# Taking the row sums of a matrix-vector product from VectorE's fused multiply-and-sum and giving the sum to ScalarE, in a float32 transformer stack on one core

## The reference, cut to what matters

```python
# first block, feed-forward: D_FF = 2816
h = rmsnorm(x, norm_ffn_g[l])
u = causal_dwconv(h @ w_up[l], ffn_conv_w[l], ffn_conv_b[l])     # 3 taps over the tokens
val, gt = jnp.split(u, 2, axis=-1)
x = x + (jax.nn.gelu(gt) * val) @ w_down[l]

# third block: 9 * 1024 = 9216 outputs from 1024 inputs
mod = (jax.nn.silu(c) @ w_ada[l] + b_ada[l]).reshape(b_, N_SUB, 3, D_MODEL)
```

## Time and profile before

| what | value |
|---|---|
| median of 3 runs | 3217.38 us (3214.98 to 3224.53) |
| the profiled execution: its time, its span | 3212.26 us, 3210.5 us |
| busy over the span: PE, DVE, ACT, POOL | 85%, 42%, 28%, 27% |
| DVE busy from 670 to 1050 us | 351.0 of 380.0 us |
| PE busy from 670 to 1050 us, granted clock | 340.2 of 380.0 us, 0.94 |
| ACT busy from 670 to 1050 us | 66.9 of 380.0 us |
| POOL busy from 670 to 1050 us | 133.3 of 380.0 us |

### The profile page before, as it was taken

The page is one execution under the profiler, slowest core; times in us unless marked ns, Lnnn a source line. Parts: engine busy times, 40 slices in busy tenths (PEclk is TensorE's granted clock), DMA queues, the critical chain, the costliest instruction groups (busy, mean ns, idle before and its releaser), DMA issues.

```text
span 3210.5 us, 30605 instructions
## 1 busy us (share of the span) xinstructions
PE 2715.9 (85%) x11642; PEld 2080.2 (65%) x11642; DVE 1344.4 (42%) x1924; ACT 910.6 (28%) x1089; POOL 882.5 (27%) x193
## 2 busy tenths in 40 slices
PE   6858588889998889998977669999978886799996
PEld 5636377677776668675754446888857543578885
DVE  3471522399999530554223442222243113323223
ACT  3322321311111333554334332212232212222211
POOL 2202033333333223111331113444413100244441
PEclk9968689999999989999988889999989766899998
DMA  3102012344444212100221002222221100122221
GB/s 125 59 14 73 20 66 92 118 158 157 160 178 161 89 43 89 40 27 27 79 79 38 28 27 73 97 91 105 91 69 66 40 13 1 53 81 103 91 98 46
DMA packets 34801, 246.00 MB, mean 77 GB/s; under 512 B 3823, under 2 KB 3823, under 8 KB 5780
## 3 DMA queue, kind: packets, MB, share of 16 engines
q1 hardware_dynamic: 33120, 240.16, 20.6%
q10 hardware_dynamic: 1588, 4.55, 0.4%
HBM read 242.58 MB, written 2.11 MB: 76 GB/s over the span
## 4 chain that ended last, share of the span: by engine, by line
issue 64%; PE 21%; POOL 11%; DVE 3%; DVEq 1%; POOLq 0%; ACT 0%; ACTq 0%
POOL WL L259 11%; PE PS L294 5%; PE PS L296 5%; PE PS L295 5%; PE PS L639 1%; PE PS L744 1%; PE PS L742 1%; PE PS L631 1%; PE PS L745 1%; PE PS L340 0%; DVE COLS L1600 0%; DVE ARENA L1681 0%; DVE ARENA L1610 0%; DVEq L1223 0%; PE PS L759 0%
## 5 line engine op out<-in xcount | busy, mean ns | idle before, releaser
L259 POOL TENSOR_TENSOR WL<-WT,WH 128x2048 fp32r<-128x2048 f32 x189 | 882.3, 4668 | 2276.9 <-ACT WH L786 1660.0
L294 PE MATMUL PS<-HH,WH 128*128 128x512 f32 x1848 | 747.3, 404 | 105.4 <-DVE ARENA L1246 39.4
L295 PE MATMUL PS<-HL,WH 128*128 128x512 f32 x1848 | 735.1, 398 | 0.0
L296 PE MATMUL PS<-HH,WL 128*128 128x512 f32 x1848 | 733.8, 397 | 0.0
L294 PEld LDWEIGHTS PS<-HH,WH 128*128 128x128 f32 x1848 | 356.7, 193 | 213.1 <-issue 100.8
L296 PEld LDWEIGHTS PS<-HH,WL 128*128 128x128 f32 x1848 | 356.4, 193 | 76.6
L295 PEld LDWEIGHTS PS<-HL,WH 128*128 128x128 f32 x1848 | 357.3, 193 | 71.9 <-issue 1.3
L294 PE MATMUL PS<-YH,WH 128*128 128x512 f32 x864 | 345.1, 399 | 50.6 <-DVEq L1185 23.2
L295 PE MATMUL PS<-YL,WH 128*128 128x512 f32 x864 | 340.6, 394 | 0.0
L296 PE MATMUL PS<-YH,WL 128*128 128x512 f32 x864 | 340.1, 394 | 0.0
L984 ACT CAST WH<-WT 128x2048 fp32r<-128x2048 f32 x90 | 171.7, 1908 | 534.9 <-PE PS L294 534.9
(11 more groups left out here) (216 smaller groups left out, 2867.3 us busy)
## 6 DMA issues: line engine op xcount, KB each, us to landing
WT<-weights SPq DMA_DIRECT2D x189, 1024.0 KB, 4.8
ARENA<-w_ada SPq DMA_DIRECT2D x36, 1024.0 KB, 6.8
X<-x_fm ACTq DMA_DIRECT2D x4, 512.0 KB, 9.4
out_fm<-X SPq DMA_DIRECT2D x1, 2048.0 KB, 6.3
ARENA<-rel_rows ACTq DMA_DIRECT2D x1, 1024.0 KB, 5.4
CON<-constants SPq DMA_DIRECT2D x1, 704.0 KB, 6.0
ARENA<-rows SPq DMA_DIRECT2D x1, 512.0 KB, 5.7
ARENA<-p_fm SPq DMA_DIRECT2D x1, 512.0 KB, 6.6
```

The lines of the kernel that those rows point to most:

```text
L259: nc.gpsimd.tensor_tensor(WL[s][:, :], WT[s][:, :], WH[s][:, :].bitcast(F32), ALU.subtract).then_inc(sem("w_lo"), 1)
L294: i0 = nc.tensor.matmul(o, w[0], r[0], start=first, stop=False, skip_group_check=True)
L295: nc.tensor.matmul(o, w[0], r[1], start=False, stop=False, skip_group_check=True)
L296: i2 = nc.tensor.matmul(o, w[1], r[0], start=False, stop=last, skip_group_check=True)
```

## The change

`ada` on DVE becomes a plain multiplication in place, `w = w * CROW`, with a semaphore step. The sum goes to ACT: a new function `sums(step, js)` waits for the multiplication and copies the piece onto itself with an accumulator whose output is the column of `MOD`; the second piece of each pair releases the buffer. The six-column copy is gone, and DVE waits for all 36 releases before it uses `MOD`. In the loop ACT's order is new: pieces 4 and 5 are summed between the first and the second cast, the gelus come after the third cast instead of before it, and pieces 0 to 3 are summed after the gelus.

```diff
--- before.py
+++ after.py
@@ -977,6 +977,14 @@
                             b = (t0 + q) % 2
                             free(f(GE[:, q, :], psb(b), ACT.Silu), b)
 
+                def sums(step, js):
+                    for j in js if conv else ():
+                        w = ADA[j // 2][:, D * (j % 2):D * (j % 2) + D]
+                        act.wait_ge(sem("ada_mul"), 6 * step + j + 1)
+                        i = f(w, w, ACT.Copy, accum_out=MOD[:, bass.ds(6 * step + j, 1)])
+                        if j % 2:
+                            i.then_inc(sem("ada_used"), 1)
+
                 def hi(k, gk):
                     s = gk % 2
                     act.wait_ge(sem(f"w_dma{s}"), w_base(k, gk))
@@ -993,6 +1001,7 @@
                 else:
                     high(g0 + 2, g0 % 2)
                     mid(0)
+                    sums(0, range(4))
                 with act.Fori(0, (CH - 1) // 2) as i:
                     for h in range(2):
                         c = 2 * i + h
@@ -1000,12 +1009,15 @@
                         hi(g + 1 + 6 * i, g + 1)
                         if not conv:
                             mid(c + 1)
-                            hi(g + 2 + 6 * i, g + 2)
-                        else:
-                            hi(g + 2 + 6 * i, g + 2)
+                        sums(c, (4, 5))
+                        hi(g + 2 + 6 * i, g + 2)
+                        hi(g + 3 + 6 * i, g + 3)
+                        if conv:
                             mid(c + 1)
-                        hi(g + 3 + 6 * i, g + 3)
+                            sums(c + 1, range(4))
+                sums(CH - 1, (4, 5))
                 next_panel(g0 + 3 * CH - 1)
+                sums(CH, range(6))
                 tiles[0] = t0 + 4 * CH
                 n["ge"] = e0 + 2 * CH
                 if conv:
@@ -1442,13 +1454,7 @@
                     if e == 0:
                         dve.wait_ge(sem(f"ada_dma{s}"), 16 * step + 16)
                     w = ADA[s][:, D * e:D * e + D]
-                    i = nc.vector.tensor_tensor_reduce(out=w, in0=w, in1=CROW, scale=1.0, scalar=0.0, op0=ALU.mult, op1=ALU.add,
-                                                       accum_out=COLS[:, 8 + j:9 + j])
-                    if e == 1:
-                        i.then_inc(sem("ada_used"), 1)
-                    if j == 5:
-                        dve.drain()
-                        nc.vector.tensor_copy(MOD[:, bass.ds(6 * step, 6)], COLS[:, 8:14])
+                    tt(w, w, CROW, ALU.mult).then_inc(sem("ada_mul"), 1)
 
                 def up(c):
                     if conv_on:
@@ -1522,7 +1528,7 @@
                 n["down"] = down0 + CH
 
             ffn(lambda k: par("norm_ffn", k), None, True, X)
-            dve.drain()
+            dve.wait_ge(sem("ada_used"), NADA)
             tt(MOD[:, :], MOD[:, :], PAR[:, POFF["b_ada"]:POFF["b_ada"] + 72], ALU.add)
             dve.drain()
             for s in range(3):
```

## The result

The changed kernel takes 3233.3 us (median of 6 runs, 3232.0 to 3234.8) against 3219.9 us for the kernel before (median of 6, 3215.0 to 3224.5): a ratio of 1.004, 95% interval 1.0028 to 1.0052, so 13 us slower. The prediction was 3236 us, in a range of 3212 to 3248, with 0.68 for slower by over 0.3%. The two profiled executions stand 19.5 us apart (spans of 3230.0 and 3210.5 us).

The account below looks back on a forecast made before the run. PE waits for DVE, which POOL's runs hold, in the first block's feed-forward stage. Nine periods +14.4, start -2.5, last chunk +1.1 and end +6.0 sum to +19.0 on the median 3217.4: 3236 us, range 3212 to 3248.

Parts of the forecast that it names:

- The holds: Pieces on DVE: the plain multiplication is held beside POOL's runs like the fused instruction; piece 3 lasts about 3.9 us.
- The rival of 3170 us: Pieces on DVE: the multiplication isn't held beside POOL and takes 1.2 us; ten chunks -53, 3170 us; chance 0.06.
- The replay: One loop chunk from PE's restart: POOL's second run holds piece 3, PE stalls 3.4 us; 39.6 us against 38.0.
- the case of 3203 us: A faster case concerning the hold of the product in the loop, 3203 us; chance 0.06.
- The fall of the clock at the new stall: PE at `down`'s fifth tile: the 3.4 us stall lowers the clock, costing 1.6 us more a chunk.
- a sign of being wrong: PE in the loop: a stall of 3 us without slow matmuls behind it would speak against the forecast.
- the first rival: Loop: the clock doesn't fall at the new stall, chunks take 38.0 us; +0.6 in sum, 3218 us; chance 0.20.
- the rival of longer falls: Loop: clock falls last longer or come twice a chunk; nine periods 22.5, sum +27, 3244 us; chance 0.15.
- The term of nine periods: Nine periods of the loop, each 1.6 us longer: +14.4 us.
- The start: Start of the stage: four sums delay POOL, DVE's product runs unheld, PE restarts at 663.3 instead of 665.77: -2.5 us.
- The last chunk: Last restart to down(10): piece 5, free before, now ends at +28.9; 32.4 us against 31.3: +1.1.
- The end: Next layer's first tiles: ACT's copy comes 4.4 us later, PE stalls, the clock falls: +6.0, between +3 and +8.

Follow-up runs that it names:

- e7: The changed kernel with the broadcast row written into PSUM, so each multiplication has one input in SBUF: 3184.9 us, ratio 0.9908 to the kernel before.
- e1: The changed kernel with the gelus again before the third cast: 3219.4 us, ratio 0.9998 to the kernel before.
- e2: The kernel before with only the third cast moved ahead of the gelus: 3250.3 us, ratio 1.0098 to the kernel before.
- e5: The changed kernel with piece 3's multiplication moved behind the first four additions of `down`: 3182.5 us, ratio 0.9903 to the kernel before.
- e6: The kernel before, fused instruction kept, with the third cast before the gelus and piece 3 behind the first four additions: 3193.3 us, ratio 0.9931.
- e9: The kernel before, fused instruction kept, with the row in PSUM, piece 5 next to piece 4 and the third cast before the gelus: 3171.6 us.
- e8: e7 with piece 5 next to piece 4 and the stage's last two sums behind the third and fifth copy: 3162.8 us, ratio 0.9835.

## Why the prediction was right, point by point

**The holds.** That the plain multiplication is held as the fused instruction was rested on one row, and is shown: 4.73 and 4.27 us, and by e7 the cause. The rival of 3170 us fell.

**The chunk.** The replay gave POOL's second run at +13.3 (measured +13.4), piece 3 at +15.2 (+14.8), the additions at +18.9 (+19.0), a stall to +19.7 (+19.75), free pieces 4 and 5, a held product, a period of 39.6 (39.8 on the mean of nine: 358.1 / 9). In that period the part from the product to the restart rests on no run: which of the two engines goes first when POOL's third run starts in the midst of the product was not shown. Measured in the chunk above, POOL's run starts at +29.1, the two multiplications of the product last from +28.6 to +34.3, the casts behind them take 0.76 us for two, the first convolution starts at +36.4, and PE restarts at +39.2 after 1.50 us. So the product is held, and the case of 3203 us fell too. e1 and e2 show that the order on ACT is the cause, e5 that it works through the late first addition.

**The fall of the clock at the new stall.** Taken as given in the forecast, it came in nine of ten chunks; one stall of 3.15 us had none (726.26 us), which the prediction had named as a sign of being wrong, and there the period is 37.8 us, as the first rival said. Two falls cost 2.9 us (periods of 40.7 and 40.7), as the rival of longer falls said. The forecast's 1.6 us for a fall are the 12.5 us of the 48 matmuls behind the restart less the 10.9 us of the next 48 (755.20 - 742.71 and 766.08 - 755.20); behind the nine stalls the changed kernel loses 1.4 to 1.7 us seven times and 3.0 twice (spacings as in e2). Which fall comes and how long it lasts is not explained by any run here; that the missing one and the two long ones nearly cancel, so that the nine periods come near 1.6 us a fall, is luck. The term of nine periods was +14.4 and measured +12.7, since the kernel before takes 38.4 us on the mean of nine and not 38.0: two of its periods have a long fall too (39.25 and 39.35) and the first is 38.85.

**The start** was -2.5 and measured -3.5, with the mechanism as told (PE waits for the panel, 3.80 us). **The last chunk** was +1.1 and measured +0.9.

**The end** is right in sum, +6.0 for +5.4, and wrong in its split. Foretold was a stall of over 4.4 us at the third tile and a fall behind it, 1.6. Measured is a stall of 2.44 us without a fall there; a held piece that ends 1.4 us later; and a fall behind the eighth tile's 2.22 us stall, some 1.6 us. The first copy came 5.4 us later behind down(10)'s start than before, but PE was later at its third tile too, by the other two parts, and so waited only 2.44. That the parts add up to nearly the forecast term is luck.

**The sum** was +19.0 and is +15.4 in the stage, +19.5 in the spans of the two traces and +13.4 in the medians. The spans differ from the medians by the rest of the program, which moves by 13 us from one execution to another. The total, 3236 against 3233.3 us, looks closer than the change does, because the kernel before measured 3219.9 us with the changed one and not the 3217.4 that the sum starts from: 2.5 us of luck.

## What to carry to other kernels

Before moving an instruction on an engine that only feeds another, place the run that it triggers on the timeline of the engine which that run can hold: here a cast that came 5 us earlier moved a hold from a piece behind the first additions to one ahead of them, and so delayed the release of a PSUM bank. Instructions that free PE's banks belong ahead of those that can be held; and an input that lies in PSUM takes a VectorE multiplication out of GpSimd's way (1.22 us at most in e7 and e9, up to 5.53 with both inputs in SBUF in the changed kernel). Either of these took 51 to 54 us off the changed kernel's stage (e5, e7). The division of the work by itself was worth less: 3.6 to 6.5 us of the stage in three pairs (before and e1, e6 and e5, e9 and e8), and 13.9 in the fourth (e2 and the changed kernel), where the falls of the clock are not the same.

## What the runs showed of the hardware

- A stall's length alone doesn't decide whether PE's clock falls. In the changed kernel nine stalls of 3.15 us were followed by matmuls of 0.63 us and one was not; one of 2.22 us was, which the earlier trace rows had not let me expect, as were five of 1.9 us out of eighteen in e2 and e6.
- A fall costs 1.3 to 2.9 us (periods of 39.2 to 40.7 in the changed kernel against 37.8 without one). In e2, with a period of 41.0 us, the long ones came eight times in a row.
- VectorE multiplications of 128x1024, plain (e7) and fused (e9), took 1.21 to 1.22 us with one input in PSUM, all 72, of which 35 and 34 ran beside GpSimd; with both in SBUF they took up to 5.5. Casts within SBUF were held as well (two in 5.18 us).
- Additions that read one input from PSUM passed beside GpSimd's run too: four in 2.49 us in e5.
- The part of the program that no experiment touches took 2747.8 to 2761.3 us in twelve profiled executions.
